# Differential attention in blocks of one query tile, with all its projections ahead of the first step

## The chip, the cores and the metric

The kernel runs on one core of one Trainium2 chip. The metric is the device time of the whole program in microseconds. The engines are TensorE (PE, with its weight load shown as PEld), VectorE (DVE), ScalarE (ACT), GpSimd (POOL) and SyncE (SP), which here only issues transfers. They have a queue each and meet at semaphores.

## The reference

Two layers of a hybrid mixer work on 1024 sample tokens (8 tiles of 128) and 128 prompt tokens (a ninth tile). Each layer normalises the input, projects it, runs four groups of heads (latent attention "mla", grouped-query attention "gqa", differential attention "diff", a long convolution "hy"), gates each with a SiLU and projects the result. The sample's queries see 128 cached keys and the 1024 of the sample, nine key tiles; the prompt's see only their own tile. The part in question is this:

```python
def diff_blocks(q, k, v, lam):
    scale = q.shape[-1] ** -0.5
    def blk(qb):
        s = jnp.einsum('bqhsd,bkhsd->bhsqk', qb, k).astype(jnp.float32) * scale
        p = jax.nn.softmax(s, axis=-1)
        a = (p[:, :, 0] - lam * p[:, :, 1]).astype(v.dtype)
        return jnp.einsum('bhqk,bkhd->bqhd', a, v)
    return over_query_blocks(blk, q)
...
    o_diff = diff_blocks(dq, k_d.reshape(b, -1, DIFF_HEADS, 2, DIFF_HD), v_d, lam)
    o_diff = (rmsnorm(o_diff, lp['diff_subln']) * (1.0 - lam_init)).reshape(b, n, GROUP_W)
```

There are four differential heads of width 64, each with two maps of width 32. Everything is float32.

## The kernel before

One layer is a sequence of stages that all engines end together (`stage_end`): input, hyena, mla, gqa, diff0, diff1, out. diff0 and diff1 hold two of the four differential heads each. Each has a **preparation** and an **attention**.

In the preparation PE projects queries and keys tile by tile (`proj`, 8 products of 256 columns, K = 1024 in eight parts), ACT copies them out, DVE turns them by the rope table and splits them (`split`), PE transposes them and ACT stores them as `q_parts` and `k_parts`. A product with float32 operands stands in the trace as two records. At the end of it stand the values of the prompt's tile (diff0 only, for both groups at once, 256 columns) and the first of three parts of the SiLU gate (`PARTS`: 512, 512 and 128 tokens).

In the attention the work is cut into **units**: one head of one query tile with its two maps. A **block** is two query tiles and two heads, so four units; the prompt's tile is a block of two short units. That gives 18 units in 5 blocks. All engines walk the same steps g = 0, 1, ...; in step g

- PE multiplies the scores of unit g, map 0 and map 1, into banks 0 to 2 and 3 to 5 of PSUM (three chunks of 384 keys each), and map m waits until the exponential of the same map of unit g-1 has read its banks;
- DVE takes a maximum over each map (`maxima`), and ACT the exponential of each with its sum (`exps`);
- DVE mixes the two maps of unit g-1 into one weight (`mix`, with the ratio of the sums and lambda), so that the result is short of the division by the first map's sum;
- PE transposes the mixed weights of units g-2 and g-3 in pieces of four, four and one key tile (`turn`) into banks 6 and 7, and ACT copies each piece to SBUF (`take`);
- three steps after a block's last unit PE multiplies it by the values (`values`): nine key tiles, two heads, two halves of 32 columns, 36 products with 32 weight columns and 256 moving columns into four column groups of bank 7. Behind them `spread_sums` brings the reciprocal sums across (4 products), ACT copies these (`spread_out`), DVE multiplies and squares (`finish`), PE sums the squares of each head with `halves` one step later (`head_squares`), ACT takes logarithm and exponential (`head_roots`), DVE scales by gain and gate (`head_norm`).

`fills` is a table of further work inside the steps: in diff0 the projection of the values of eight sample tiles (steps 0 to 4, two, two, two, one, one) and gate parts 1 and 2, in diff1 the gate parts only. Each gate part inside the steps makes ACT load the table for tanh and load the one for exp again. `late` and `turn_bank` move a unit's pieces around such steps. The queue of SP loads the rope table (`ROPE_DIFF`) first in diff0 and keeps it for diff1. All this is written out by hand; the order within an engine is the order of the code.

The lines that the prediction's steps touch:

```python
QUERY_TILES = [(0, 1), (2, 3), (4, 5), (6, 7), (NT,)]
...
    if grp == "diff0" and g < 5:
        return [("v", t) for t in ((0, 1), (2, 3), (4, 5), (6,), (7,))[g]]
```

Of the kernel before, what the change touches and what calls it, by code (L numbers as in the profile page):

```python
# [60 lines left out]
            ("diff", 0): ("proj", "diff1", NT), ("diff_vg", 0): ("gate", "diff", 1, 2)}  # L61
# [44 lines left out]
DD = PT + 5 * 1152  # L106
DQ, RS, RB, ROPE_DIFF = DD + GW, DD + 2 * GW, DD + 3 * GW, DD + 4 * GW
LAMQ, LAMP = ROPE_DIFF + 512, ROPE_DIFF + 640
# [15 lines left out]
ROPE_GQA = SPLIT + 2 * 896  # L124
# [16 lines left out]
QUERY_TILES = [(0, 1), (2, 3), (4, 5), (6, 7), (NT,)]  # L141
BLOCKS = {g: [(tiles, p) for tiles in QUERY_TILES for p in range(len(PAIRS[g]))] for g in PAIRS}
# [36 lines left out]
def piece_engine(grp, u, j):  # L179

    if MAPS[grp] == 2:
        return "scalar"
    return ("scalar", "vector", "vector")[j]
# [12 lines left out]
def late(grp, g):  # L196

    return bool(due(grp, g) or MAPS[grp] == 2 and fills(grp, g))


def turn_bank(grp, u, j):

    if fills(grp, u + 2):
        return 6
    return (6, 7, 6)[j] if due(grp, u + 2) else (7, 6, 7)[j]


def slot(grp, u):

    n, i, ti = UNITS[grp][u]  # L210
    return (n % 2) * 4 * (NSLOT[grp] == 8) + 2 * i + ti


def fills(grp, g):

    if grp == "diff0" and g < 5:
        return [("v", t) for t in ((0, 1), (2, 3), (4, 5), (6,), (7,))[g]]
    if grp == "diff0":
        return {7: [("gate", 1, slice(0, 2))], 8: [("gate", 1, slice(2, 5))], 9: [("gate", 1, slice(5, KD))],
                13: [("gate", 2, slice(0, KD))]}.get(g, [])  # L220
    if grp == "diff1":
        return {0: [("gate", 1, slice(0, 3))], 1: [("gate", 1, slice(3, 6))], 2: [("gate", 1, slice(6, KD))],
                4: [("gate", 2, slice(0, KD))]}.get(g, [])
    return []
# [16 lines left out]
class Signals:  # L241
# [3 lines left out]
    ONCE = ("constants", "x_copied", "silu_ready", "exponent_set", "layer_finished", "semaphores_cleared", "layer_entered", "ones_set")  # L245
# [94 lines left out]
def program(nc, I, outs, known=None):  # L340
    with ExitStack() as ctx:
# [44 lines left out]
        eps = sb("eps", [P, 1])  # L386
# [16 lines left out]
        def stage_value(k):  # L403
            return S.raw("stage_done"), 4 * k
# [19 lines left out]
        def _(sp):  # L424
# [9 lines left out]
            with sp.Fori(0, DEPTH) as l:  # L434
# [114 lines left out]
                load(at(ROPE_DIFF, NT, 64), I["rope"][:, :, 0:64], "diff_params")  # L549
# [52 lines left out]
        def _(pe):  # L602
# [14 lines left out]
            with pe.Fori(0, DEPTH) as l:  # L617
# [133 lines left out]
                def gate(grp, c, c0, f, i, banks, ks=slice(0, KD)):  # L751
# [3 lines left out]
                    ps = claim(("gate", grp, f, i), banks) if ks.start == 0 else bank[banks[0]]  # L755
                    for k in range(KD)[ks]:
                        last = mm(ps[:, 0:n], W[:, SLOT[c, 0], k, c0 + f * P:c0 + (f + 1) * P],
                                  hT[:, k, tok:tok + n], k == 0, k == KD - 1)
                    if ks.stop == KD:
                        last.then_inc(*K.done(("gate", grp, f, i)))  # L760

                def diff_values(t, banks):

                    weights("diff_vg")
                    ps = claim(("v", "diff", t), banks)
                    for k in range(KD):
                        last = mm(ps[:, 0:GW], hT[:, k, t * P:(t + 1) * P], W[:, SLOT["diff_vg", 0], k, 0:GW],
                                  k == 0, k == KD - 1)
                    last.then_inc(*K.done(("v", "diff", t)))
# [66 lines left out]
                def attention(grp):  # L836


                    units, diff = UNITS[grp], MAPS[grp] == 2
                    steps = tail_step(grp)  # L840
# [13 lines left out]
                    def scores(u, s, chunk=None):  # L854

                        n, i, ti = units[u]
                        tiles, p = BLOCKS[grp][n]
                        t, m = tiles[ti], 2 * i + s if diff else PAIRS[grp][p][i]
                        x = MAPS[grp] * u + s
# [1345 lines left out]
```

## Time and profile before

| | before |
|---|---|
| median of 3 runs | 2740.0 us (2735.8 to 2743.5) |
| profiled execution | 2737.1 us, its span 2734.9 us |
| instructions | 33688 |
| PE, PEld busy | 2426.1 us, 1596.1 us |
| DVE, ACT busy | 1319.2 us, 943.0 us |
| mean granted clock of PE | 0.942 |

The busy time of an engine is a mean over stages that have different limits, so it is read by stretch. The table by stretches has for each engine the busy time and the number of its instructions, then the granted clock of PE (1.00 is 2.4 GHz, 0.50 is 1.2 GHz) and the share of the transfer queues. The timeline has start and duration of each merged run of instructions and, in brackets, how long the engine idled ahead of it and who ended that.

### The profile page before, as it was taken

Reading aid. Unit: us, or ns where it says so; the run is one execution under the profiler, and the core shown is the slowest. Engines: PE = TensorE matmul, PEld = TensorE weight load, DVE = VectorE, ACT = ScalarE, POOL = GpSimd, SP = SyncE. Lnnn points to the kernel's source line nnn. Section 1 sums busy time; section 2 is a strip of 40 time slices with the busy share of each in tenths; the row PEclk is TensorE's granted clock in tenths of the full one; section 3 lists DMA queues with packets and bytes.
Section 4 is the critical chain, followed back from the end, with each engine's and each line's share of the span. In section 5 each row is a group of like instructions: output and inputs, shape, how many; then the busy total and the mean of one; then the engine's idle time right before and its main releaser. Section 6 shows DMA issues by size and latency. Waiting matters only on the chain. (4 is left out here: it accounts for less than half of the span.)

```text
span 2734.9 us, 33688 instructions
## 1 busy us (share of the span) xinstructions
PE 2426.1 (89%) x13152; PEld 1596.1 (58%) x13152; DVE 1319.2 (48%) x2658; ACT 943.0 (34%) x1886; POOL 172.8 (6%) x184
## 2 busy tenths in 40 slices
PE   3999999899898987879859999999988989888798
PEld 1765765674476756554327567557745667565543
DVE  3352664564364474661133426545553644746611
ACT  2242113541253364651022421135412533646510
POOL 0120000001000000001202200010010000000012
PEclk8999999999999998989969999999999989989799
DMA  6430100100100000102155101000001000001021
GB/s 216 165 140 26 50 16 1 48 1 13 58 7 9 3 1 2 63 1 91 60 178 213 61 26 50 16 21 29 1 13 64 1 9 3 1 2 63 1 93 61
DMA packets 72136, 128.42 MB, mean 47 GB/s; under 512 B 22915, under 2 KB 36099, under 8 KB 70341
## 3 DMA queue, kind: packets, MB, share of 16 engines
q1 hardware_dynamic: 71864, 121.52, 13.0%
q10 hardware_dynamic: 112, 4.72, 0.5%
q8 instruction: 108, 1.77, 0.3%
q14 instruction: 52, 0.42, 0.1%
HBM read 109.02 MB, written 21.92 MB: 48 GB/s over the span
## 5 line engine op out<-in xcount | busy, mean ns | idle before, releaser
L609 PE MATMUL psum<-arena 128*32 128x256 f32 (+8 forms) x8496 | 1743.0, 451 | 123.8 <-DMA arena<-in_hy_decay 46.9
L609 PEld LDWEIGHTS psum<-arena 128*32 128x32 f32 (+3 forms) x8496 | 1013.1, 161 | 780.7 <-issue 526.3
L613 PE MATMUL psum<-ident,arena 128*128 128x128 f32 (+1 forms) x2248 | 366.6, 291 | 76.2 <-ACT arena L1284 30.0
L1763 DVE TENSOR_REDUCE st<-psum 128x1 f32<-128x1152 f32 (+1 forms) x288 | 352.0, 1235 | 137.1 <-PE psum L609 135.5
L1469 DVE TENSOR_TENSOR arena<-arena 128x64 f32<-128x64 f32 (+10 forms) x686 | 304.5, 490 | 175.8 <-ACT arena L1420 57.5
L613 PEld LDWEIGHTS psum<-ident,arena 128*128 128x128 f32 (+1 forms) x2248 | 268.1, 146 | 178.6 <-issue 59.7
L1268 ACT ACTIVATE arena<-psum,st 128x1152 f32<-128x1152 f32 (+1 forms) x288 | 324.8, 1129 | 118.8 <-DVE st L1763 115.3
L609 PE MATMUL psum<-k_parts,q_parts 96*128 96x384 f32 (+2 forms) x1000 | 300.4, 391 | 34.4 <-ACT arena L1268 22.9
L1284 ACT COPY arena<-psum 128x512 f32<-128x512 f32 (+1 forms) x344 | 170.6, 505 | 230.3 <-PE psum L613 229.2
L1469 DVE TENSOR_TENSOR arena<-psum,arena 128x512 f32<-128x512 f32 (+2 forms) x136 | 75.1, 553 | 355.6 <-PE psum L609 308.2
L609 PEld LDWEIGHTS psum<-k_parts,q_parts 96*128 96x128 f32 (+1 forms) x1000 | 181.5, 205 | 53.3 <-ACT arena L1268 36.6
L2016 POOL TENSOR_TENSOR st<-st,mhalf 128x1 f32<-128x1 f32 (+2 forms) x72 | 56.1, 779 | 1467.0 <-DVE st L1474 1467.0
L1777 DVE COPY arena<-psum 128x512 f32<-128x512 f32 (+1 forms) x256 | 116.0, 481 | 33.0 <-PE psum L613 33.0
L1469 DVE TENSOR_TENSOR st<-st 128x1 f32<-128x1 f32 x18 | 2.9, 160 | 213.5 <-ACT arena L1454 213.5
L1420 ACT COPY arena<-psum 128x256 f32<-128x256 f32 (+1 forms) x54 | 22.0, 408 | 241.8 <-PE psum L609 216.1
L2016 POOL TENSOR_TENSOR arena<-arena 128x1024 f32<-128x1024 f32 (+2 forms) x38 | 89.3, 2358 | 245.9 <-DVE arena L1597 217.3
L1454 ACT ACTIVATE arena<-psum 128x512 f32<-128x512 f32 x36 | 21.5, 597 | 229.0 <-PE psum L609 229.0
L1790 DVE SCALAR_TENSOR_TENSOR arena<-arena,st 128x1152 f32<-128x1152 f32 (+1 forms) x72 | 93.6, 1300 | 2.5
L1628 DVE SCALAR_TENSOR_TENSOR arena<-arena,hcw 128x1024 f32<-128x1024 f32 x24 | 30.8, 1285 | 121.4 <-ACT arena L1181 121.0
L613 PE MATMUL psum<-ident,split_buf 128*96 128x128 f32 (+1 forms) x456 | 62.9, 282 | 25.1 <-DVE split_buf L1469 24.6
L613 PEld LDWEIGHTS psum<-ident,split_buf 128*96 128x96 f32 (+1 forms) x456 | 51.6, 132 | 44.7 <-DVE split_buf L1469 38.1
L609 PE MATMUL psum<-k_parts,q_low 96*128 96x384 f32 (+1 forms) x200 | 68.9, 345 | 0.0
(125 smaller groups left out, 1170.1 us busy)
## 6 DMA issues: line engine op xcount, KB each, us to landing
arena<-in_ada_w SPq DMA_DIRECT2D x12, 2048.0 KB, 9.0
arena<-in_w_in SPq DMA_DIRECT2D x10, 2048.0 KB, 9.0
arena<-out_xs SPq DMA_DIRECT2D x36, 512.0 KB, 4.7
out_xs<-arena SPq DMA_DIRECT2D x18, 512.0 KB, 2.6
arena<-in_w_out SPq DMA_DIRECT2D x4, 2048.0 KB, 7.9
out_xs<-in_x ACTq DMA_DIRECT2D x1, 4608.0 KB, 17.3
spectrum_kept<-arena SPq DMA_DIRECT2D x2, 2304.0 KB, 8.4
arena<-spectrum_kept SPq DMA_DIRECT2D x2, 2304.0 KB, 8.8
```

Of the source, the lines that this page charges most:

```text
L609: return nc.tensor.matmul(out, lhsT, rhs, start=start, stop=stop)
L613: return nc.tensor.transpose(out, src, ident[0:n, 0:n])
L1268: nc.scalar.activation(at(buf, nk, w), psum[:, 512 * b0:512 * (b0 + nk)].rearrange("p (c n) -> p c n", c=nk)[:, :, 0:w], ACT.Exp, bias=st[ ...
L1284: nc.scalar.copy(at(SLOTS[grp] + slot(grp, u) * 1152 + 512 * j, nk * P), bank[b][:, 0:nk * P]).then_inc(*S.up("turned_scalar", (grp, number)))
L1420: ins = nc.scalar.copy(at(z, nz), B(job)[:, 0:nz])
L1454: nc.scalar.activation(at(YN + 2 * D, 512), B(job), ACT.Square, accum_out=st[:, 8 * (t % 2) + half:8 * (t % 2) + half + 1]).then_inc(*S.up ...
L1469: return nc.vector.tensor_tensor(out, a, b, op)
L1628: ins = [nc.vector.scalar_tensor_tensor(at(c, D), at(u + shift * P, D), hcw[:, f, tap:tap + 1], at(c, D), ALU.mult, ALU.add), nc.vector.sc ...
L1763: nc.vector.tensor_reduce(st[:, 16 + x % 4:17 + x % 4], psum[:, 512 * b0:512 * (b0 + nk)].rearrange("p (c n) -> p c n", c=nk)[:, :, 0:w], ...
L1777: nc.vector.tensor_copy(at(SLOTS[grp] + slot(grp, u) * 1152 + 512 * j, nk * P), bank[b][:, 0:nk * P]).then_inc(*S.up("turned_vector", (grp ...
L1790: nc.vector.scalar_tensor_tensor(p0, p1, c, p0, ALU.mult, ALU.add).then_inc(*S.up("mixed", (grp, u)))
L2016: return nc.gpsimd.tensor_tensor(out, a, b, op)
```

## The change

Query blocks of the differential groups become one tile wide (9 blocks of two units), with attention functions of their own. Values are taken two steps apart, 36 products of 128 columns each. The products that spread the sums, ACT's copy of them and DVE's product with them are gone: the mean square of the unscaled result is compared with epsilon times the square of the sum, which enters the same bank by a product with the identity, so the first sum cancels. The norm is done for four blocks at once (`HEADS_NORMED`). Four buffers of weights instead of three are in turn. The values of the sample are projected in the preparation of each group, 128 columns a group, and all three gate parts too; `fills` is gone. The rope table is loaded in both stages, behind the other parameters.

```diff
-QUERY_TILES = [(0, 1), (2, 3), (4, 5), (6, 7), (NT,)]
-BLOCKS = {g: [(tiles, p) for tiles in QUERY_TILES for p in range(len(PAIRS[g]))] for g in PAIRS}
+QUERY_TILES = {1: [(0, 1), (2, 3), (4, 5), (6, 7), (NT,)], 2: [(t,) for t in range(TT)]}
+BLOCKS = {g: [(tiles, p) for tiles in QUERY_TILES[MAPS[g]] for p in range(len(PAIRS[g]))] for g in PAIRS}
+HEADS_NORMED = ((0, 4), (4, 8), (8, 9))
...
 def turn_bank(grp, u, j):
     if MAPS[grp] == 2:
-        return "scalar"
+        return (7, 6, 7)[j] if u % 2 else (6, 6, 7)[j]
...
-                load(at(ROPE_DIFF, NT, 64), I["rope"][:, :, 0:64], "diff_params")
...
                 for part in range(2):
                     if part == 1:
                         sp.wait_ge(*stage_value(5))
+                    load(at(ROPE_DIFF, NT, 64), I["rope"][:, :, 0:64], "diff_rope", part)
...
+                def sample_values(grp, half):
+                    job, c = ("v", grp, half), P * int(grp[4])
+                    ps = claim(job, K.next())
+                    for i in range(4):
+                        t = 4 * half + i
+                        for k in range(KD):
+                            last = mm(ps[:, i * P:(i + 1) * P], hT[:, k, t * P:(t + 1) * P],
+                                      W[:, SLOT["diff_vg", 0], k, c:c + P], k == 0, k == KD - 1)
+                    last.then_inc(*K.done(job))
...
+                    def head_squares(b):
+                        n0, n1 = HEADS_NORMED[b]
+                        pe.wait_ge(*S.at("head_squares", (grp, b)))
+                        take_bank(7, S.at("roots_begun", (grp, b)))
+                        mm(bank[7][:, 0:(n1 - n0) * P], halves[:, :], at(DQ, (n1 - n0) * P), True, False)
+                        for k in range(n1 - n0):
+                            last = mm(bank[7][:, k * P:(k + 1) * P], at(TH["diff"] + k * P, P), ident[:, :],
+                                      False, k == n1 - n0 - 1)
...
+                    for g in range(steps):
+                        if g < len(units):
+                            scores(g, 0)
+                        if g % 2:
+                            turn(g - 3, 1)
+                        if g < len(units):
+                            scores(g, 1)
+                        for b in normed(g - 1):
+                            head_squares(b)
+                        turn(g - 3, 2)
+                        if g % 2:
+                            turn(g - 2, 1)
+                        turn(g - 2, 0)
+                        for n in due(grp, g):
+                            values(n)
...
                     if grp[:4] == "diff":
-                        gate("diff", "diff_vg", GW, int(grp[4]), 0, K.next())
+                        for i in range(3):
+                            gate("diff", "diff_vg", GW, int(grp[4]), i, K.next())
+                        for half in range(2):
+                            sample_values(grp, half)
...
+                    for g in range(tail_step(grp)):
+                        take(g - 3, 0)
+                        take(g - 3, 1)
+                        if g % 2 == 0:
+                            take(g - 3, 2)
                         if g < len(units):
                             exps(g, 0)
+                        for b in normed(g - 1):
+                            head_roots(b)
+                        if g % 2:
+                            take(g - 3, 2)
+                        if g < len(units):
+                            exps(g, 1)
...
                     for g in range(tail_step(grp)):
                         if g < len(units):
+                            maxima(g, 0)
+                            maxima(g, 1)
+                        if 0 <= g - 1 < len(units):
+                            mix(g - 1)
+                        for b in normed(g - 2):
+                            head_norm(b)
+                        for n in due(grp, g):
+                            if n >= 4 and n % 4 == 0:
+                                v.wait_ge(*S.at("normed", (grp, n // 4 - 1)))
+                            read_out(n)
+                        for b in normed(g):
+                            squares(b)
```

PE's queue at the end of diff0's preparation, before: the prompt's values (the 256 columns), the first gate part, the last transposes. L609 is the helper that multiplies, L613 the one that transposes; `arena` holds nearly all tiles in SBUF.

```order
L609 MATMUL psum<-arena 128x256 [waits bank0_drained,weights1_loaded]
L609 MATMUL psum<-arena 128x256 x7
L609 MATMUL psum<-arena 128x512 [waits bank1_drained,weights1_loaded]
L609 MATMUL psum<-arena 128x512 x7
L613 MATMUL psum<-ident,split_buf 96x128 [waits bank2_drained,split]
```

The same place after (the helpers stand at L600 and L604):

```order
L600 MATMUL psum<-arena 128x256 x7
L600 MATMUL psum<-arena 128x512 [waits bank1_drained,weights1_loaded]
L600 MATMUL psum<-arena 128x512 x7
L600 MATMUL psum<-arena 128x512 [waits bank2_drained,weights1_loaded]
L600 MATMUL psum<-arena 128x512 x7
L600 MATMUL psum<-arena 128x128 [waits bank3_drained,weights1_loaded]
L600 MATMUL psum<-arena 128x128 x7
L600 MATMUL psum<-arena 128x128 [waits bank4_drained]
L600 MATMUL psum<-arena 128x128 x31
L600 MATMUL psum<-arena 128x128 [waits bank5_drained]
L600 MATMUL psum<-arena 128x128 x31
```

Gate parts 1 and 2 and 64 products of 128 columns for the values have come here from the steps.

PE's queue around the first block's values, before (step 6 of diff0):

```order
L609 MATMUL psum<-k_parts,q_parts 128x384 [waits exps]
L609 MATMUL psum<-k_parts,q_parts 128x384 x2
L609 MATMUL psum<-arena 32x256 [waits turned_scalar,bank7_drained]
L609 MATMUL psum<-arena 32x256 x35
L609 MATMUL psum<-ident,st 64x128 [waits inverse_sums]
L609 MATMUL psum<-ident,st 64x128 x3
L613 MATMUL psum<-ident,arena 128x128 [waits turned_scalar,mixed]
L613 MATMUL psum<-ident,arena 128x128 x3
```

After (step 4 of diff0):

```order
L600 MATMUL psum<-k_parts,q_parts 128x384 [waits exps]
L600 MATMUL psum<-k_parts,q_parts 128x384 x2
L604 MATMUL psum<-ident,arena 128x128 [waits turned_scalar,mixed] x2
L604 MATMUL psum<-ident,arena 128x128 x3
L600 MATMUL psum<-arena 32x128 [waits bank5_drained,turned_scalar,bank0_drained]
L600 MATMUL psum<-arena 32x128 x35
L600 MATMUL psum<-k_parts,q_parts 128x384 [waits exps]
L600 MATMUL psum<-k_parts,q_parts 128x384 x2
```

The block has half the columns in as many products and comes twice as often; the products with the sums are gone, and the transposes of the next unit stand ahead of the values.

DVE's queue in the last block of diff1, before: maxima (L1763), the mix (L1787 to L1790), and `finish` (L1469).

```order
L1763 TENSOR_REDUCE st<-psum 128x1 [waits scores] x2
L1787 RECIPROCAL st<-st 128x1 [waits exps]
L1788 SCALAR_TENSOR_TENSOR st<-st,lamv 128x1 [waits vector_step]
L1790 SCALAR_TENSOR_TENSOR arena<-arena,st 128x1152 [waits vector_step]
L1469 TENSOR_TENSOR arena<-psum,arena 128x256 [waits normed,spread_out,sums_spread]
L1469 TENSOR_TENSOR arena<-arena 128x256 [waits read_out]
```

After, a step with a block due:

```order
L1906 TENSOR_REDUCE st<-psum 128x1 [waits scores] x2
L1915 RECIPROCAL st<-st 128x1 [waits exps]
L1916 SCALAR_TENSOR_TENSOR st<-st,lamv 128x1 [waits vector_step]
L1918 SCALAR_TENSOR_TENSOR arena<-arena,st 128x1152 [waits vector_step]
L1923 COPY arena<-psum 128x128 [waits values]
```

DVE no longer waits for ACT's copy of the sums, and takes one copy of 128 columns out of the bank instead of a product and a square of 256.

## Rows read from the trace of the kernel before

**Rows 1.** The page, busy time, share of the span and instructions

```profile
PE 2426.1 (89%) x13152; PEld 1596.1 (58%) x13152; DVE 1319.2 (48%) x2658; ACT 943.0 (34%) x1886; POOL 172.8 (6%) x184
```

**Rows 2.** Busy time by stretch, first layer: diff0 preparation, attention, diff1 preparation, attention

```profile
872.99:930.05 57.06, 51.82 (x253) 42.15 (x253) 23.40 (x113) 16.42 (x33) 0.00 (x0) 0.97 0.06 14
930.05:1067.19 137.14, 110.09 (x748) 78.91 (x748) 81.03 (x117) 78.37 (x152) 0.00 (x0) 0.90 0.00 1
1067.19:1117.49 50.30, 48.34 (x236) 39.23 (x237) 22.54 (x107) 15.78 (x31) 0.00 (x0) 0.97 0.13 45
1117.49:1234.74 117.25, 87.25 (x620) 60.79 (x620) 80.41 (x117) 75.25 (x144) 0.00 (x0) 0.82 0.06 19
```

**Rows 3.** diff1, eight units by stretch; the timeline of ACT, units 0, 1 and 16

```profile
1160.14:1209.97 49.83, 37.47 (x286) 25.99 (x285) 37.66 (x51) 32.64 (x63) 0.00 (x0) 0.83 0.00 1
...
1119.68 1.22 ACT L1268 ACTIVATE arena<-psum,st 128x1152 f32<-128x1152 f32 x1 [1.39 <-DVE st L1763]
...
1123.32 1.22 ACT L1268 ACTIVATE arena<-psum,st 128x1152 f32<-128x1152 f32 x1 [1.07 <-DVE st L1763]
...
1215.55 0.37 ACT L1268 ACTIVATE arena<-psum,st 128x128 f32<-128x128 f32 x1
```

**Rows 4.** Timeline of DVE in diff1, the maxima of two units in a row

```profile
1171.21 2.59 DVE L1763 TENSOR_REDUCE st<-psum 128x1 f32<-128x1152 f32 x2
...
1175.49 2.62 DVE L1763 TENSOR_REDUCE st<-psum 128x1 f32<-128x1152 f32 x2
```

**Rows 5.** Timeline of diff1, DVE behind a block's values, PE ahead of a block's squares

```profile
1207.72 0.42 DVE L1469 TENSOR_TENSOR arena<-psum,arena 128x256 f32<-128x256 f32 x1 [2.96 <-ACT arena L1298]
...
1189.10 0.67 PE L609 MATMUL psum<-arena,halves 128*128 128x256 f32 x2 [2.90 <-ACT arena L1284]
```

**Rows 6.** Timeline, 512 columns (weight load, output stage); 2 columns with 128 weight columns

```profile
1241.04 0.19 PEld L609 LDWEIGHTS psum<-arena 128*128 128x128 f32 x1 [0.24 <-issue]
...
116.35 3.73 PE L609 MATMUL psum<-sel,arena 128*128 128x2 f32 x32
```

**Rows 7.** Timeline of diff1, the first scores, and a hand-over at full clock

```profile
1117.49 1.30 PE L609 MATMUL psum<-k_parts,q_parts 96*128 96x384 f32 x6 [1.17 <-DVE arena L1650]
...
1193.65 1.23 ACT L1268 ACTIVATE arena<-psum,st 128x1152 f32<-128x1152 f32 x1
...
1195.03 0.79 PE L609 MATMUL psum<-k_parts,q_parts 96*128 96x384 f32 x3 [0.78 <-ACT arena L1268]
...
1195.79 1.33 DVE L1763 TENSOR_REDUCE st<-psum 128x1 f32<-128x1152 f32 x1
```

**Rows 8.** diff0's preparation: issue and landing of the rope table, then the timeline

```profile
arena<-in_rope SPq DMA_DIRECT2D x1, 256.0 KB, 3.4
...
881.10 0.42 DVE L1469 TENSOR_TENSOR arena<-arena 128x32 f32<-128x32 f32 x2 [8.22 <-DMA arena<-in_cache_diff_v]
...
884.60 0.64 PE L613 MATMUL psum<-ident,split_buf 128*96 128x128 f32 x4 [3.01 <-DVE split_buf L1469]
```

**Rows 9.** Timeline of PE in diff1, values of two tiles and of the prompt's

```profile
1152.68 4.09 PE L609 MATMUL psum<-arena 128*32 128x256 f32 x72
1156.70 0.66 PE L609 MATMUL psum<-ident,st 128*64 128x128 f32 x8
...
1229.58 0.43 PE L609 MATMUL psum<-arena 128*32 128x128 f32 x8
...
1229.94 0.44 PE L609 MATMUL psum<-ident,st 128*64 128x128 f32 x4
```

**Rows 10.** Groups by line and form, whole span: VectorE on 512 columns

```profile
L1469 DVE TENSOR_TENSOR arena<-arena 128x512 f32<-128x512 f32 x36 | 23.0, 683 | 0.0
```

**Rows 11.** Busy time by stretch in diff1, and three scores at the low clock

```profile
1170.00:1176.00 6.00, 3.01 (x17) 2.26 (x18) 5.89 (x10) 4.41 (x11) 0.00 (x0) 1.00 0.00 0
1176.00:1180.00 4.00, 4.00 (x39) 1.85 (x41) 3.82 (x5) 2.85 (x6) 0.00 (x0) 0.57 0.01 4
...
1164.39 1.52 PE L609 MATMUL psum<-k_parts,q_parts 96*128 96x384 f32 x3
```

More of the change, by code:

```diff
@@ L210, in slot, with normed @@
     n, i, ti = UNITS[grp][u]
+    if MAPS[grp] == 2:
+        return 2 * (n % 2) + i
     return (n % 2) * 4 * (NSLOT[grp] == 8) + 2 * i + ti
[L214 to L224, printed above, removed]
+def normed(g):
+    return [b for b, (n0, n1) in enumerate(HEADS_NORMED) if g == 2 * (n1 - 1) + 4]
 def tail_step(grp):
@@ L836, in attention @@
                 def attention(grp):
-                    units, diff = UNITS[grp], MAPS[grp] == 2
-                    steps = tail_step(grp)
+                    units, steps = UNITS[grp], tail_step(grp)
                     turned_by = {}
@@ L961, in attention @@
                                 turn(g - 3, 2)
-                        if diff:
-                            if new:
-                                scores(g, 1)
-                            if last_turn and behind:
-                                turn(g - 3, 2)
-                        for job in fills(grp, g):
-                            run_fill(job)
                         for n in burst:
@@ L1304, in attention @@
                         take(g - 3, 2)
-                        if not diff and not late(grp, g):
+                        if not late(grp, g):
                             take(g - 2, 0)
                         if g < len(units):
-                            exps(g, 0)
-                        if diff:
-                            if not late(grp, g):
-                                take(g - 2, 0)
-                            if g < len(units):
-                                exps(g, 1)
-                            for n in due(grp, g):
-                                spread_out(n)
-                            for job in fills(grp, g):
-                                if job[0] == "v":
-                                    keep_values(job[1])
+                            exps(g)
@@ L1319, in attention @@
                         if late(grp, g):
                             take(g - 2, 0)
-                        elif diff:
-                            take(g - 2, 1)
-                        for job in fills(grp, g):
-                            if job[0] == "gate" and job[2].stop == KD:
-                                gate_tanh("diff", int(grp[4]), job[1], [(int(grp[4]), i) for i in range(3)])
-                                nc.scalar.preload_act_table_set("natural_log_exp_and_others")
-                        if diff:
-                            for n in due(grp, g - 1):
-                                head_roots(n)
@@ L1833, in attention @@
                         if g < len(units):
-                            for m in range(MAPS[grp]):
-                                maxima(g, m)
-                        if not diff:
-                            for n in due(grp, g):
-                                finish(n)
+                            maxima(g)
+                        for n in due(grp, g):
+                            finish(n)
                         if not late(grp, g):
                             take(g - 2, 1)
-                        mix(g - 1)
-                        for job in fills(grp, g - 1):
-                            if job[0] == "gate" and job[2].stop == KD:
-                                f = int(grp[4])
-                                gate_finish("diff", f, job[1], [(f, i) for i in range(3)], OT + 4 * TOK)
                         for n in range(len(BLOCKS[grp])):
@@ L1978, in _ @@
                         f = int(grp[4])
[L1979 removed]
+                        for i in range(3):
+                            gate_finish("diff", f, i, [(f, i) for i in range(3)], OT + 4 * TOK)
                     if grp == "diff0":
```

322 lines of the change are left out of this document (192 added, 130 removed).

## The prediction

> **What bounds the kernel now.** I read the page first: TensorE is busy for 89% of the span [rows 1], so the question is whether it is busy on the path in the two differential stages. The table by stage [rows 2] gives their four parts in each layer: preparation 57.06 us and attention 137.14 us for diff0, preparation 50.30 us and attention 117.25 us for diff1, 361.75 us together. The second layer runs the same instructions, and I take it to last as long. In the preparations PE is busy for 91 and 96% and sets the pace. In the attentions it is busy for 80 and 74%, with the granted clock at 0.90 and 0.82: there no engine is full, and the time is a ring of waits. diff0 is 19.9 us longer than diff1 because the values' projection fills its first steps.
>
> The ring, in the stretch of diff1 without fills: eight units (a unit is one head of one query tile, with two maps) take 49.83 us, 6.2 us each [rows 3]. VectorE's own work for a unit, two maxima and a mix, repeats after 4.28 us (1171.21 to 1175.49) [rows 4]. So 1.9 us of each unit are lost, most of it in the step where PE multiplies two tiles of values in one piece and VectorE sits idle for 2.96 us, and in the next, where PE idles for 2.90 us ahead of the product with halves [rows 5].
>
> **Term 1, work moved into the preparation.** Per group, gate part 1 (512 tokens, 16 records) goes at 0.43 us a record, a weight load of 0.19 and the 0.24 ahead of it in such a stream: 6.8 us [rows 6]. Gate part 2 (128 tokens) is 16 records of 128 columns. Their price at full clock comes from 32 products with 128-column weights and almost no columns, 3.73 us, 0.117 us each [rows 6]. That makes 1.8 us. The values' projection is no longer 128 records of 256 columns once but, per group, 128 records of 128 columns at 0.115 to 0.117 us: 14.8 us, since the weight load now covers the columns. Sum 23.4 us a group, all of it on the path, since PE sets the pace there; ACT's and VectorE's shares (three tanh, two copies, three gate products) run beside it except for the last copy. I take off 0.8 us a group, because the first scores no longer wait for a tanh and a gate product (1.17 us idle [rows 7]).
>
> **Term 2, the rope table** is now loaded behind the eight others instead of ahead of them in diff0. Before, VectorE started at 881.10, freed by the values' cache, and PE waited 3.01 us for its split. The new load is issued at about 878.9, where the values' cache load ends on SP's queue, and lands 3.4 us later, at 882.3: 1.2 us a layer, PE waiting [rows 8]. In diff1 the same load is issued with the stage, and VectorE starts only when 5.4 us later the first projection has been copied: hidden; without that cover it would cost 3.4 us.
>
> Preparations after, per layer: 57.06 + 50.30 + 46.8 + 1.2 - 1.6 = 153.8 us. So the attention part A, alike in both groups now, has to be (361.75 - 153.8) / 2 = 104.0 us for an even exchange; every microsecond of A counts four times.
>
> **Term 3, a pair of units.** I laid the new order out over two steps with hand-overs from the rows: first score to maximum 0.76 us (1195.03 to 1195.79), exponential to the next score 1.38 (1193.65 to 1195.03) [rows 7]. Unknown is the price of the values: 36 products of 32 weight columns by 128, 72 records. The only such rows are the prompt's blocks, 8 records, and the product behind them starts 0.36 us later, 0.045 us each with the fill in it: 3.2 us for 72. From below, 256 columns cost 4.02 us for 72 records (1152.68 to 1156.70) [rows 9], so half the columns cannot cost less than 2.0 us. I take 2.6 us, the middle, since the eight records hold a start that 72 pay once. Counted from the first maximum of an even step: VectorE has done both maxima and the mix at 4.3 us. PE sets off the second map's scores at 0.0, turns the last piece and the next unit's first (which waits for ACT's two copies, until 0.9), and begins the values at 1.35. They end at 3.95 (4.55 with 3.2 us), and 0.5 us later the read-out can start: 4.45, against 4.3 on VectorE. This is the wait that the change adds: VectorE's read-out of a block stands in every even step ahead of the next unit's maxima, and the next scores stand behind the values on PE. The read-out takes 0.25 us (128 columns, a good third of the 0.68 us of 512 [rows 10]). In the odd step PE's flips follow ACT's copies one by one through banks 6 and 7; the last is done at 8.15, the next scores reach VectorE at 8.9, and VectorE itself is through at 9.0. So a pair takes 9.0 us (9.6 with 3.2 us for the values, 8.85 with 2.0), and PE, ACT and VectorE all arrive within 0.3 us of each other. The per-block steps that are gone (spreading the sums, ACT's copy, finishing and rooting per block) are what made the idle time.
>
> Work of the norm that remains, once within the steps: squares, product, norm, four VectorE operations of 512 columns at 0.68 us and a little more [rows 10], 3.0 us.
>
> **Term 4, the clock.** The granted clock fell to 0.50 (1.2 GHz) after sparse stretches: 1170 to 1176 had PE busy for 3.0 of 6.0 us at 1.00, and 1176 to 1180 stood at 0.57 [rows 11]. Three scores that take 0.79 us at 2.4 GHz take 1.52 at the low level [rows 7, 11]. Two such hand-overs (0.73 us each), the flips on the path (0.8 us) and the values, whose streaming doubles (1.2 us), make 3.5 us, less what slack there is: 3.2 us more for a pair at 1.2 GHz. Before, the clock over the stretch is 0.83, a third of its time low [rows 3]. After, the 2.9 us gaps are gone, the longest left is about 1.5 us, so I take a quarter: 0.8 us a pair.
>
> **Term 5, ends.** Start 2.2 us (first scores to first exponential, 1117.49 to 1119.68) and 16.5 us for the first four steps (3.64 and three of 4.28) [rows 3, 7]. The tail from unit 16's exponential took 19.2 us (1215.55 to 1234.74) [rows 2, 3]. After, PE has block 6's values in front (2.6 us) and unit 15's three pieces can only follow the copies of unit 14's: they are in SBUF at 7.8 us. Then the values of block 7 take 2.6, read-out and squares 1.9, product with halves and epsilon 2.1, the two roots 1.3, norm 1.5, and the last block's short chain 4.0 behind it; with 0.8 for the clock 22 us.
>
> **Sum.** A = 2.2 + 16.5 + 6 x 9.0 - 0.9 (unit 16 is short) + 3.0 + 6 x 0.8 + 22 = 101.6 us. Against 104.0 that is -2.4 x 4 = -9.6 us. The profiled execution took 2737.1 us (span 2734.9), 2.9 under the median of 2740.0, so I forecast 2727.5 us.
>
> A page of the Trainium skill speaks against this change. "TensorE: Matmul & The Clock Gate", section "Back-to-back issue gap", gives about 81 ns for each pair of weight load and product with 128 columns in a sustained stream. By that, 72 records would be 5.8 us and the time about that of the last rival below. The trace disagrees: 0.045 us a record where eight stand in a row.
>
> **Rivals.** (a) *Cheap values and full clock*: 2.0 us and no low clock give pairs of 8.85 and a tail of 20, A = 2.2 + 16.5 + 53.1 - 0.9 + 2.9 + 20 = 93.8, 2696 us; the case covers 2690 to 2716. For it: no gap over 1.5 us is left; against it: the odd step leaves PE busy for about half its time, as 1170 to 1176 was. Chance 0.26.
> (b) *The clock, slower than before.* Place: the value block on PE after a sparse odd step. If it stays low for a third of the time (1.07 a pair) and values cost 3.2 us (9.6 a pair), A = 2.2 + 16.5 + 57.6 - 0.9 + 3.0 + 6.4 + 23.5 = 108.3, 2754 us; it decides from A = 104.0. Chance 0.26.
> (c) *The steps do not shorten*: some wait takes the place of the removed ones (ACT now takes three pieces ahead of an exponential, each bound to one bank), and a unit stays at 6.2 us: A = 2.2 + 16.5 + 74.4 - 0.9 + 22 = 114, 2778 us. For it: bank 7 serves flips, values and norm; against it: my layout leaves 0.3 us or more at each. Chance 0.09.
> (d) *Issue pace*: the 64-column products take 0.66 us for eight, 0.082 each taken whole [rows 9]; at that pace values are 5.9 us, a pair 12.3, A = 128, 2833 us. Chance 0.03.
>
> **How the numbers follow.** Forecast case (2716 to 2738) 0.36, its sides split at 2728.9: 0.20 below, 0.16 above. About 0.3%, 8.2 us, is what a measurement of this kernel can tell from no change. Faster: 0.20 + 0.26 = 0.46. Same: 0.16 + 0.08 from (b) = 0.24. Slower: 0.18 + 0.09 + 0.03 = 0.30. The range 2698 to 2780 leaves out the far end of (a), some 0.1, and (d) with the worst of (c), another 0.07; the forecast's own is 2716 to 2738.
>
> **What would show it.** Preparations of about 80 us (diff0) and 73 us (diff1), with 128-column records at 0.115 us; both attentions of equal length near 102 us; pairs near 9.8 us; the 72 value records between 2.0 and 3.2 us at full clock; VectorE busy for over 85% between units 4 and 15; a granted clock over 0.85. Wrong it would be if the attention is above 104 us with the clock at 0.8, or if VectorE waits for values in each even step.

## The result and the profile after

The changed kernel took 2711.65 us, the median of 4 runs (2705.65 to 2715.74), against 2740.6 us before in the same session: ratio 0.9894, 95% interval 0.9871 to 0.9918. It is faster by 22 to 35 us. I had forecast 2727.5 us, 12.5 us less than the 2740.0 us known before.

The page's busy line, after:

```profile
PE 2423.7 (89%) x14472; PEld 1625.8 (60%) x14472; DVE 1318.3 (49%) x2642; ACT 909.3 (34%) x1826; POOL 172.8 (6%) x183
```

TensorE has 1320 more records than in [rows 1] (a product of float32 operands stands as two) and is busy for as long; the page alone does not tell where time went. The table by stretch does. The same four parts as in [rows 2], first layer of the changed kernel (length, PE, PEld, DVE, ACT, POOL busy, then granted clock):

```profile
875.73:956.56 80.83, 75.39 (x413) 61.76 (x413) 24.30 (x114) 18.02 (x37) 0.00 (x0) 0.97 0.04 10
956.56:1055.84 99.28, 75.05 (x854) 57.63 (x854) 79.79 (x112) 66.58 (x129) 0.00 (x0) 0.85 0.01 1
1055.84:1129.64 73.80, 72.15 (x396) 58.97 (x397) 23.52 (x109) 17.53 (x35) 0.00 (x0) 0.97 0.11 35
1129.64:1228.38 98.74, 74.65 (x854) 57.19 (x855) 79.41 (x111) 66.61 (x129) 0.00 (x0) 0.86 0.06 23
```

The preparations grew by 23.8 and 23.5 us, the attentions fell by 37.9 and 18.5 us; in the second layer by the same reading +23.6, +22.7, -38.1 and -18.0 us. Over both layers that is 725.3 us before and 706.4 us after, -18.9 us; my sum had -9.6. The attentions are now alike, at 98.7 to 99.3 us, where I had 101.6.

The stretch that answers to [rows 3], eight units of diff1, and behind it four more:

```profile
1150.30:1188.09 37.79, 31.43 (x418) 24.07 (x418) 36.22 (x47) 31.32 (x58) 0.00 (x0) 1.00 0.01 2
...
1188.09:1208.02 19.93, 15.05 (x199) 11.61 (x198) 18.45 (x28) 15.00 (x29) 0.00 (x0) 0.90 0.01 2
```

Eight units take 37.79 us for 49.83, with the first part of one batch of the norm among them, at a clock of 1.00 for 0.83. VectorE is busy for 96% of it. This is no longer a ring of waits: VectorE binds, as the run with half of the values shows below. ACT's exponentials for units 4, 6, 8, 10, 12, 14 and 16 in the timeline give the pairs:

```profile
1150.30 1.22 ACT L1362 ACTIVATE arena<-psum,st 128x1152 f32<-128x1152 f32 x1
...
1159.19 1.22 ACT L1362 ACTIVATE arena<-psum,st 128x1152 f32<-128x1152 f32 x1 [0.44 <-DVE st L1906]
...
1168.08 1.22 ACT L1362 ACTIVATE arena<-psum,st 128x1152 f32<-128x1152 f32 x1 [0.44 <-DVE st L1906]
...
1176.97 1.22 ACT L1362 ACTIVATE arena<-psum,st 128x1152 f32<-128x1152 f32 x1 [0.45 <-DVE st L1906]
...
1188.09 1.22 ACT L1362 ACTIVATE arena<-psum,st 128x1152 f32<-128x1152 f32 x1 [0.32 <-DVE st L1906]
...
1198.42 1.22 ACT L1362 ACTIVATE arena<-psum,st 128x1152 f32<-128x1152 f32 x1
...
1208.02 0.37 ACT L1362 ACTIVATE arena<-psum,st 128x128 f32<-128x128 f32 x1
```

Three pairs take 8.89 us each; then come 11.12 us with the norm's squares, product and roots in it, 10.33 us with its last two operations, 9.60 us for the pair that ends at the short unit. Inside a pair at full clock, PE's rows and VectorE's:

```profile
1159.15 2.17 PE L600 MATMUL psum<-arena 128*32 128x128 f32 x72
1161.25 0.79 PE L600 MATMUL psum<-k_parts,q_parts 96*128 96x384 f32 x3
...
1160.72 1.42 DVE L1918 SCALAR_TENSOR_TENSOR arena<-arena,st 128x1152 f32<-128x1152 f32 x1
1162.05 0.28 DVE L1923 COPY arena<-psum 128x128 f32<-128x128 f32 x1
1162.25 2.69 DVE L1906 TENSOR_REDUCE st<-psum 128x1 f32<-128x1152 f32 x2
```

The 72 records of a block's values take 2.10 us to the next start, 0.029 us each, where I had 2.6 for the block. The scores behind them are there at 1162.04, and VectorE comes to them at 1162.25: it does not wait here, TensorE is 0.2 us early. The idle times of [rows 5], 2.96 us of VectorE and 2.90 us of PE, have no successor in these pairs.

### The profile page after: what moved, and what is told of

Read it like the earlier page. It is cut to its first block and busy times, and to the rows that moved or that the text cites. A ratio compares the mean times of both kernels' runs of the same rounds, so it can differ in the third digit from the quotient of the medians.

```text
span 2714.0 us, 36345 instructions
## 1 busy us (share of the span) xinstructions
PE 2423.7 (89%) x14472; PEld 1625.8 (60%) x14472; DVE 1318.3 (49%) x2642; ACT 909.3 (34%) x1826; POOL 172.8 (6%) x183
## 5 line engine op out<-in xcount | busy, mean ns | idle before, releaser
L600 PE MATMUL psum<-arena 128*32 128x128 f32 (+8 forms) x9904 | 1730.4, 405 | 115.5 <-DMA arena<-in_hy_decay 46.3
L600 PEld LDWEIGHTS psum<-arena 128*128 128x128 f32 (+3 forms) x9904 | 1047.4, 155 | 738.2 <-issue 516.7
L604 PE MATMUL psum<-ident,arena 128*128 128x128 f32 (+1 forms) x2248 | 362.7, 287 | 91.6 <-ACT arena L1376 41.5
L604 PEld LDWEIGHTS psum<-ident,arena 128*128 128x128 f32 (+1 forms) x2248 | 262.0, 144 | 196.1 <-issue 100.9
L600 PE MATMUL psum<-k_parts,q_parts 96*128 96x384 f32 (+2 forms) x1000 | 302.6, 393 | 34.3 <-ACT arena L1362 21.0
L600 PEld LDWEIGHTS psum<-k_parts,q_parts 96*128 96x128 f32 (+1 forms) x1000 | 181.9, 208 | 59.9 <-ACT arena L1362 35.9
L1554 DVE TENSOR_TENSOR arena<-psum,arena 128x512 f32<-128x512 f32 (+2 forms) x116 | 67.2, 580 | 278.6 <-PE psum L600 278.2
```

Source lines behind the costliest of these rows:

```text
L600: return nc.tensor.matmul(out, lhsT, rhs, start=start, stop=stop)
L604: return nc.tensor.transpose(out, src, ident[0:n, 0:n])
L1554: return nc.vector.tensor_tensor(out, a, b, op)
```

## The experiments

"The four differential parts" below are both preparations and both attentions in both layers of one profiled execution. They repeat closely: 725.3 and 725.0 us before, 706.4 and 706.5 us after. Five variants were executed once only, so I read their parts and not their totals: 2760.50 us without the sums' chain, 2734.22 with the norm for each block, 2768.86 with twice the values, 2712.64 with half, 2734.77 for the kernel before. In the diffs, `...` stands for lines left out.

**The changed kernel once more.**

> The changed kernel once more, timed in five rounds. Its profile has the four differential parts 18.9 us shorter than before, while the medians differ by 29 us. If the stages are all there is, the ratio to the kernel before comes near 0.993 (19 us) and every other stage lasts as long in both kernels within about 2 us. If something outside the differential stages also got faster, the ratio stays near 0.989 and another stage shows some 8 us less in both traces of the changed kernel.

Measured: 2711.97 us against 2740.18, ratio 0.9891 (0.9875 to 0.9908). So the 28 us are real: they came twice. But neither of the two readings holds: the differential parts give 18.8 us as before, and the rest of the span is 2007.6 and 2009.3 us in the two traces of the changed kernel, 2009.6 and (below) 2007.6 us in those of the kernel before.

**The move alone, with the blocks of before.** In the kernel before:

```diff
 def fills(grp, g):
-    if grp == "diff0" and g < 5:
-        return [("v", t) for t in ((0, 1), (2, 3), (4, 5), (6,), (7,))[g]]
...
     return []
...
-                        gate("diff", "diff_vg", GW, int(grp[4]), 0, K.next())
+                        for i in range(3):
+                            gate("diff", "diff_vg", GW, int(grp[4]), i, K.next())
+                    if grp == "diff0":
+                        for t in range(NT):
+                            diff_values(t, K.next())
```

> The kernel before with only the move: all gate parts and the values of the eight sample tiles (256 columns, once) in the preparation, the steps without fills, blocks of two tiles and the norm per block as before. If the blocks and the norm bring the gain and the move costs: preparation of diff0 57.1 + 8.6 + 29.0 - 0.8 = 93.9 us, of diff1 50.3 + 8.6 - 0.8 = 58.1 us, a unit still 6.2 us, both attentions 2.2 + 16.5 + 12 x 6.2 - 0.9 + 19.2 = 111.4 us, a layer 374.8 us against 361.75, so about 26 us slower than before: 2767 us. If the fills in the steps were what kept the ring slow, both attentions come near 100 us and the kernel is about 2721 us.

Measured: 2757.72 us, ratio 1.0062 (1.0041 to 1.0082), differential parts 743.6 us, 18.3 more than before. Preparations 93.44 and 59.15 us, attentions 111.07 and 108.79 us in the first layer. The first theory holds to about 2%. Over both layers the attentions lose 69.9 us by it and the preparations gain 88.1, so the move alone costs time.

**The same, and the chain of the sums gone** (two-tile blocks, norm per block):

```diff
-                        spread_sums(n, u0, len(tiles))
+                        if not diff:
+                            spread_sums(n, u0, len(tiles))
...
-                        mm(bank[6][:, 0:nq], halves[:, :], at(DQ, nq)).then_inc(*S.up("squares_summed", (grp, n)))
+                        mm(bank[6][:, 0:nq], halves[:, :], at(DQ, nq), True, False)
+                        for ti in range(nq // P):
+                            last = mm(bank[6][:, ti * P:(ti + 1) * P], at(RB + ti * P, P), ident[:, :], False, ti == nq // P - 1)
+                        last.then_inc(*S.up("squares_summed", (grp, n)))
...
-                        link(tt(at(DD, nq), O, at(RB, nq), ALU.mult), "read_out", (grp, n))
+                        nc.vector.tensor_copy(at(DD, nq), O).then_inc(*S.up("read_out", (grp, n)))
...
```

The variant still has to bring epsilon in: TensorE adds the identity products shown above, and VectorE forms their operand in two operations of 0.24 us a block, which are among the lines left out.

> The kernel with only the move (all in the preparation, two-tile blocks), and now without the products that spread the sums, ACT's copy of them and VectorE's product with them: the block is read out by one copy of 256 columns, and epsilon times the squared sum enters the bank of squares, per block. Four attentions took 439 us with the move alone, 410 us with one-tile blocks and the norm done for each. If the one-tile blocks bring that difference, this kernel stays at 104 us or more an attention (VectorE no longer waits 2.96 us for the copy, but TensorE still holds it up by 4.1 us of values in one piece): four attentions between 415 and 439 us. If the removed chain of the sums was the whole of it, they come to about 410 us here too.

Measured: the attentions take 111.5 to 112.1 us, 446.8 in all, the differential parts 751.1 us: not a gain but 7.5 us more, outside even the first bound. A block step of diff1 with the move alone, VectorE's waits and what PE does ahead of the second:

```profile
1173.22 0.42 DVE L1469 TENSOR_TENSOR arena<-psum,arena 128x256 f32<-128x256 f32 x1 [1.75 <-ACT arena L1294]
...
1179.09 0.67 PE L601 MATMUL psum<-arena,halves 128*128 128x256 f32 x2 [2.90 <-ACT arena L1280]
...
1179.40 0.88 PE L601 MATMUL psum<-k_parts,q_parts 96*128 96x384 f32 x3
...
1180.32 2.62 DVE L1763 TENSOR_REDUCE st<-psum 128x1 f32<-128x1152 f32 x2 [1.91 <-PE psum L601]
```

and the same place without the sums' chain:

```profile
1177.24 1.19 PE L601 MATMUL psum<-arena,halves 128*128 128x256 f32 x2 [2.84 <-ACT arena L1284]
...
1178.22 1.06 PE L601 MATMUL psum<-ident,arena 128*128 128x128 f32 x4
1178.94 1.31 PE L601 MATMUL psum<-k_parts,q_parts 96*128 96x384 f32 x3
...
1171.07 0.42 DVE L1818 COPY arena<-psum 128x256 f32<-128x256 f32 x1 [0.68 <-PE psum L601]
...
1180.28 2.62 DVE L1765 TENSOR_REDUCE st<-psum 128x1 f32<-128x1152 f32 x2 [3.72 <-PE psum L601]
```

The wait for the copy (L1294) is gone and the idle time is not: 1.75 + 1.91 us became 0.68 + 3.72. PE still stands ahead of the product with halves, for 2.84 us where it was 2.90, since bank 6 is held by flipped weights that ACT copies only behind its exponentials. That part is no worse than it was. What grew is the way from this product to the scores that VectorE waits for, 3.04 us for 1.23: the identity products stand in it, and it runs at a granted clock of 0.50 where the other kernel has 1.00. So the run does not price the removal by itself, but the removal with its replacement and the clock that came with them.

**One-tile blocks, the norm for each block.** In the changed kernel:

```diff
-HEADS_NORMED = ((0, 4), (4, 8), (8, 9))
+HEADS_NORMED = tuple((n, n + 1) for n in range(TT))
```

> The changed kernel with the norm done for each block on its own, as the kernel before did, in place of four at once. If batching is a part of the gain because the norm's chain (squares, product, roots, bank 7 free again) stalls the ring each time, as the one batch does by 2.2 us, a pair takes 11.1 us and the attention about 109 us. If only VectorE's extra work counts (four operations of 128 columns, 1.2 us, in place of a quarter of 2.8), the pair takes 9.4 to 10.1 us and the attention 101 to 104 us.

Measured: differential parts 719.4 us, attentions 101.7 to 104.4 us, pairs 9.9 to 11.7 us. Batching is thus worth 13.9 us in four attentions (13.0 in the differential parts). The attentions are where the second theory had them, but most pairs are longer than its 10.1 us: it isn't VectorE's work alone, the flips behind the small product wait for ACT's roots each time:

```profile
1181.37 0.39 PE L600 MATMUL psum<-ident,arena 128*128 128x128 f32 x2
1183.97 1.37 PE L604 MATMUL psum<-ident,arena 128*128 128x128 f32 x9 [2.22 <-ACT arena L1383]
```

The chain of variants, differential parts in us: before 725.3; move alone 743.6; sums' chain gone 751.1; one-tile blocks in their new queue order 719.4; norm in batches 706.4. The third step is 31.7 us; in the attentions alone it is 36.6.

**What binds a pair: values twice, values by half.**

```diff
-                        for kt in kts:
+                        for y, kt in enumerate((kts + kts)):
...
-                                              kt == kts[0], kt == kts[-1])
+                                              y == 0, y == len((kts + kts)) - 1)
```

The second kernel has `kts[:(len(kts) + 1) // 2]` in place of `(kts + kts)`: it leaves four of the nine key tiles out of every block's sum, so it shows times and not a result.

> The changed kernel with every block's values multiplied twice over (72 products of 128 columns for 36; the sums hold each key tile twice). It asks what binds a pair of units, 8.89 us at full clock. If TensorE reaches the next scores only 0.2 us ahead of VectorE, as my layout has it, a block of 4.3 us in place of 2.17 makes the pair 10.7 to 10.9 us and an attention some 13 us longer (112 us). If VectorE alone binds and the 1.4 us that TensorE idles in a pair are free, the pair grows by 0.8 us to 9.7 us, an attention by 5 us.

> The changed kernel with only 5 of the 9 key tiles in every block's values (20 products for 36, 1.2 us; the rest of the sum is left out). If VectorE binds the pair, it stays at 8.8 to 8.9 us and the attention is at most 2 us shorter, by its tail, so that the price of the values below 2.2 us was never worth anything. If TensorE's block binds, the pair falls by up to 1 us. The granted clock tells a third thing: with TensorE less busy it should fall more often, which could make the attention longer than 99 us.

Twice, the values' rows of three blocks:

```profile
1166.64 4.14 PE L600 MATMUL psum<-arena 128*32 128x128 f32 x144
1177.34 4.14 PE L600 MATMUL psum<-arena 128*32 128x128 f32 x144
1188.04 4.14 PE L600 MATMUL psum<-arena 128*32 128x128 f32 x144
```

A pair of 10.70 us; attentions 108.5 to 113.7 us, 11.8 more on average. The first theory holds: 1.97 us more of values (4.07 for 2.10, to the next start) made the pair 1.81 us longer. By half:

```profile
1160.66 1.30 PE L600 MATMUL psum<-arena 128*32 128x128 f32 x40
1169.56 1.30 PE L600 MATMUL psum<-arena 128*32 128x128 f32 x40
1178.45 1.30 PE L600 MATMUL psum<-arena 128*32 128x128 f32 x40
```

Still 8.90 and 8.89 us, and the attentions 95.5 to 99.3 us, 1.9 less on average. So 8.9 us is VectorE's own floor, and by my estimate from these two runs the block touches it at about 2.3 us of values (4.07 less 1.81): past that point nearly each microsecond counts, below it none does within these pairs. The third question has a weak yes: the granted clock of the four attentions is 0.81 to 0.85 for 0.85 to 0.88 in the changed kernel, and the one at 0.81 is the one that did not get shorter (99.3 us).

**Part of the values back into the first steps.** The second half of a group's sample values goes into TensorE's gaps in steps 0 to 2, in bank 7, which is first used in step 3:

```diff
+def steps_fill(grp, g, s):
+    n = ((0, 12), (3, 7), (3, 7))[g][s] if g < 3 else 0
...
-                        for half in range(2):
-                            sample_values(grp, half)
+                        sample_values(grp, 0)
...
                             scores(g, 0)
+                        late_values(steps_fill(grp, g, 0))
...
                             scores(g, 1)
+                        late_values(steps_fill(grp, g, 1))
...
                             exps(g, 1)
+                        if g == 2:
+                            keep_samples(grp, 1)
```

> The changed kernel with the second half of the sample's values (4 tiles, 32 products of two records, 7.4 us) taken back out of the preparation and into the gaps of TensorE in the steps 0 to 2 of each group, where the trace shows it at the low clock with gaps of 2.3 and 1.5 us. If these gaps and the clock are free room: the preparations shorten by 7.4 us each, the first four steps stay at 18.5 us or shrink to 16.5 since the clock holds, the whole is 29 to 37 us faster than the changed kernel, about 2680 us. If the fills lengthen the steps one for one, as fills did in the kernel before, the time stays at about 2712 us.

Measured: 2682.11 us, ratio to the kernel before 0.9793 (0.9773 to 0.9812); 29.9 less than the changed kernel's in the same session; differential parts 672.5 us, 34 less. The first steps of diff1, in the changed kernel and then here:

```profile
1129.64:1148.20 18.56, 13.23 (x43) 10.07 (x44) 14.97 (x17) 12.45 (x20) 0.00 (x0) 0.58 0.31 112
```

```profile
1113.40:1132.00 18.60, 15.97 (x108) 14.65 (x109) 15.52 (x17) 13.59 (x23) 0.00 (x0) 0.92 0.32 114
```

and the fill of step 0 in PE's timeline:

```profile
1114.54 2.84 PE L606 MATMUL psum<-arena 128*128 128x128 f32 x24
1117.13 0.78 PE L606 MATMUL psum<-k_parts,q_parts 96*128 96x384 f32 x3
```

24 records in 2.59 us, 0.108 us each. The stretch is as long with the fill's 64 records in it. TensorE had stood there at 1.2 GHz, behind gaps of 2.3 and 1.5 us, and now goes at 2.4 GHz nearly throughout. The clock itself gave little here: the four steps from the first exponential to unit 4's (1115.59 to 1133.70) take 18.11 us for 18.46. In diff0, where the granted clock of these steps went from 0.55 to 1.00, they take 17.44 for 18.38. The gain is 7.1 to 7.9 us off each preparation, 29.9 in all, and the attentions are 4.0 us shorter together. Not every place gains: the pair behind the fill, from unit 4 to 6, takes 10.0 us for 8.89 in both diff1 stages.

**The same, and the rope table first again.**

```diff
                 sp.wait_ge(*stage_value(4))
+                load(at(ROPE_DIFF, NT, 64), I["rope"][:, :, 0:64], "diff_rope", 0)
...
-                    load(at(ROPE_DIFF, NT, 64), I["rope"][:, :, 0:64], "diff_rope", part)
+                        load(at(ROPE_DIFF, NT, 64), I["rope"][:, :, 0:64], "diff_rope", part)
```

> The same, and the rope table of diff0 loaded ahead of the other parameters again, as in the kernel before. If the load stood on the path as my term 2 says, TensorE waits 3.0 us for its split in place of 3.7 and more, and the whole is 1 to 2.4 us faster than the kernel with fills alone, which the times hardly tell but the preparation of diff0 does. If the load was hidden, that wait stays 3.7 us.

Measured: 2682.48 us, ratio 0.978 (0.9758 to 0.9803), differential parts 671.9 us: no difference that the times show. From the stage's first product to the first turned split it is 12.05 and 12.54 us in the two layers, 12.78 and 12.29 us without this edit, 12.90 and 12.79 in the changed kernel, 11.61 and 11.93 before. This pair does not show the size of term 2, but the rows show what VectorE's first work in diff0 waited for, without this edit in the changed kernel and with it here:

```profile
885.13 0.42 DVE L1554 TENSOR_TENSOR arena<-arena 128x32 f32<-128x32 f32 x2 [9.50 <-DMA arena<-in_rope]
...
884.45 0.42 DVE L1576 TENSOR_TENSOR arena<-arena 128x32 f32<-128x32 f32 x2 [8.65 <-DMA arena<-in_cache_diff_v]
```

All eleven traces hold this place twice. With the rope table last (six traces) VectorE begins 8.64 to 9.76 us into the stage, 9.17 on average, and each time the rope table releases it; with the table first (five traces) it begins at 8.05 to 9.04 us, 8.46 on average, released by the values' cache. The load stood on the path, for about 0.7 us.

**The kernel before, profiled again.**

> The kernel before, profiled a second time. Medians of nine runs differ by 28 us, the profiled executions of both kernels by 20 to 21 us, of which the four differential parts make 18.8. If the first profile of before was only at the fast edge of its scatter, this one shows the differential parts again at 725 us within 2 us, and the other stages up to 5 us longer. If the differential parts scatter themselves, they come out at 730 us or more.

Measured: differential parts 725.0 us, span 2732.6 us. The parts do not scatter, and the other stages are not longer. The first reading is right on the parts and wrong on the rest. The rest of the span, the same work in all kernels here, is between 2004.8 and 2014.2 us in the eleven traces.

## Why the prediction was right and where it was not

**Right**: the sign and the mechanism. The move costs and the shorter ring pays for it. The preparations: I had +46.4 us a layer, the traces give +47.3 and +46.3. The 128-column records cost 0.108 us in the fill above, near the 0.115 of term 1. Term 2 had the cause right and the size too high: 0.7 us on average over the traces where I had 1.2. That the first two profiles give 1.3 (9.40 us into the stage for 8.11) is luck.

**Wrong in size**: the attention, each microsecond of which counts four times. Diff1 of the first layer, by the terms:

| term | forecast | trace |
|---|---|---|
| start, first scores to first exponential | 2.2 | 2.20 |
| first four steps | 16.5 | 18.46 |
| six pairs | 60.9 | 57.72 |
| tail from unit 16's exponential | 22 | 20.36 |
| A | 101.6 | 98.74 |

- **Term 4, the clock, is the step that failed**: 0.8 us a pair. TensorE did fall to the low level, but in the first four steps, where VectorE sets most of the pace and it cost 0.4 us in diff1 and 0.9 in diff0 as the fills show, and once more behind the norm (0.90 from 1188.09 on). Four of the six pairs ran at 1.00. What it cost in all six, estimated from the last pair (9.60 + 0.9 - 8.89), is about 1.6 us for 4.8. Over the six pairs the granted clock is 0.965, which is the low level for 7% of the time where I had taken a quarter. I had carried the low share of the old ring over to a ring that leaves no such idle stretches.
- **Term 3**: the pair itself is 8.89 us for 9.0, because the values cost 2.1 us and not 2.6; the norm costs 3.7 us (11.12 + 10.33 - 2 x 8.89) for 3.0. My layout said 9.0 us at 2.6 us of values and held that TensorE and VectorE arrive together; the run with twice the values (10.70 us at 4.1) and the one with half (8.9 us at 1.2) bear that out within some 0.2 us.
- The price of the values was readable. [rows 9] give 256 columns at 0.056 us a record with 32 weight columns, and a 128-column weight needs 0.216 us for 256 columns (16 records in the 3.46 us from 885.51 to 888.97 of the first trace), 3.9 times as much. By the same ratio, 0.115 us gives 0.030 us, close to the 0.029 measured. I took the middle between two bounds where a ratio stood in the trace. A page of the Trainium skill, "TensorEngine Tiling (Array Packing)", section "Key Properties", says that tiles of the array can load and multiply in parallel; the ratio agrees with it. The 81 ns for each pair of weight load and product that I cited against the change from the Trainium skill, "TensorE: Matmul & The Clock Gate", section "Back-to-back issue gap", did not come about in these blocks: 0.029 us.
- **Term 5**: the first steps were 2.0 us longer. Only a part of it is the clock: with the fills, and so at 2.4 GHz nearly throughout, they still take 18.1 us here and 17.4 in diff0. The last two of the four take 4.86 and 5.16 us where I had 4.28; with the move alone, in the order of before, they take 4.37 and 4.31. In the new order the flips begin there, wait for ACT's copies (0.56 us at 1143.53) and stand ahead of scores for which VectorE then waits (1.07 us at 1145.62). The tail was 1.6 us shorter.

Rival (a) was nearest, on price and clock in the pairs, and its 2690 to 2716 us hold the median; its A of 93.8 is too low, by the first steps, the norm and the clock behind it. Rival (c) describes what the removal of the sums' chain does in two-tile blocks: there a wait did take its place. What freed the ring in the new kernel is the block that is half as long together with the new order of the queues and the fourth buffer of weights. Which of these does it I did not try apart.

**The rest of the miss.** The median is 15.9 us under the forecast. The differential parts give 9.3 of these (-18.9 for -9.6). The other 6.6 lie outside the sum, which I had set against the profiled execution before: the profiled execution of the changed kernel is 4.1 us over its median, and the rest of the span is 2.0 us shorter in this pair of traces.

**Open**: the profiled executions differ by 17 to 21 us, the medians by 28. The traces place 18.9 us in the differential parts and nothing outside them that is clear of the scatter there (2004.8 to 2014.2 us). In the same session as the second timing the unprofiled executions have a granted clock of 0.937 to 0.940 before and 0.947 to 0.949 after, the profiled ones 0.942 and 0.947 before, 0.950 and 0.947 after. So the kernel before may lose more to the clock in executions that no trace shows. That is not shown: among its eight unprofiled executions the two longest (2745.88 and 2743.73 us) have the highest clock of the eight, 0.940. Where these 9 us lie stays open.

## What to carry to other kernels

Cost a wait's removal together with what is queued next on the engine that waited: taking the sums' chain away in the old blocks lost 7.5 us, and the same with half-length blocks in a new order then brought 31.7. Where work is cut into pieces, its price for the critical engine has a knee (here 2.3 us of values in a pair of 8.9); find on which side of it you are before spending on it. And fill work belongs into steps that another engine paces, and only as much as they have room for. In the first three steps 7 us of the values' projection cost nothing. The kernel before had put about four times as much (128 records of 0.216 us) into the first five steps of diff0, and its first four steps took 33.5 us where the move alone has 17.1 to 17.4. This change had put it all where it was paid in full. The variant with half of the values back in the steps beats the kernel before by 58 us and the changed one by 30.

## What the hardware showed that I had not expected

Products with 32 weight columns for four row ranges of the output run at nearly a quarter of the price of a full-width one, for 128 columns as for 256: 0.029 and 0.056 us a record for 0.108 and 0.216. At a granted clock of 0.50 a block of 72 takes 4.00 us for 2.10 (1035.54 to 1039.54 in diff0 of the first layer), almost twice. And VectorE's floor hid most of a clock of 0.58 over 18.6 us: TensorE at half speed cost diff1 0.4 us, and diff0, at 0.55, 0.9 us.
